# Routed experts of a two-layer decoder step: first unit taken out of the loop, tokens gathered by row instead of scattered by slot

## What is computed

```python
logits = jnp.einsum('bld,de->ble', h, router)
top_p, top_i = lax.top_k(softmax(logits), 2)      # weights made to sum to 1
for e in range(8):                                 # D_MODEL 1024, D_FF_EXPERT 1408
    out = out + combine[..., e:e+1] * swiglu(h, wg[e], wu[e], wd[e])
```

## Time and profile before

| | |
|---|---|
| median of 3 runs | 2325.3 us (2324.82 to 2325.86) |
| the profiled execution | 2321.99 us, span 2320.2 us |
| PE busy | 2076.9 us (90%), mean granted clock 0.951 |
| DVE busy | 1337.7 us (58%) |
| ACT busy | 942.0 us (41%) |
| POOL busy | 322.0 us (14%) |
| read from and written to DRAM | 384.07 MB and 43.47 MB |

### The profile page before, as it was taken

How to read it: one execution, slowest core, us unless ns; L and a number is a source line. 1 busy time by engine, 2 the same in 40 slices (tenths; PEclk the granted TensorE clock), 3 DMA queues, 4 the chain that set the end, 5 groups by cost and what they waited for, 6 DMA issues and landing times.

```text
span 2320.2 us, 38053 instructions
## 1 busy us (share of the span) xinstructions
PE 2076.9 (90%) x14026; PEld 1852.4 (80%) x14026; DVE 1337.7 (58%) x1712; ACT 942.0 (41%) x1085; POOL 322.0 (14%) x306
## 2 busy tenths in 40 slices
PE   4979999999799999979889999994499999999993
PEld 2868999998699999967789999893377777777772
DVE  2655665733533232246646566426488888888884
ACT  3321222343422122143212222524466767676664
POOL 2101212200000000001011222001221111122211
PEclk9988999999899999999989999997699999999997
DMA  8532222333922222226412232310799999998993
GB/s 317 201 127 64 96 77 98 113 138 135 401 90 88 79 86 94 87 90 242 155 55 82 90 108 91 119 51 33 301 340 357 358 355 363 362 365 336 345 357 134
DMA packets 117685, 428.31 MB, mean 185 GB/s; under 512 B 7792, under 2 KB 20400, under 8 KB 117120
## 3 DMA queue, kind: packets, MB, share of 16 engines
q1 hardware_dynamic: 90912, 323.43, 38.4%
q0 software_dynamic: 26720, 104.13, 12.2%
HBM read 384.07 MB, written 43.47 MB: 184 GB/s over the span
## 4 chain that ended last, share of the span: by engine, by line
PE 61%; issue 26%; DVE 4%; POOL 3%; ACT 2%; DMA 2%; DVEq 0%; POOLq 0%; SPq 0%; ACTq 0%
PE ps L1469 48%; PE ps L1493 3%; POOL wlr L605 3%; PE ps L1483 2%; PE ps L1584 1%; PE ps L1599 1%; PE ps L1580 1%; PE ps L1506 1%; DMA raw<-w_xbc 1%; PE ps L1595 1%; PE ps L1597 1%; PE ps L1554 1%; PE ps L1596 1%; POOL h_rows L595 0%; POOL rawr L613 0%
## 5 line engine op out<-in xcount | busy, mean ns | idle before, releaser
L1382 DVE TENSOR_TENSOR wlr<-rawr,whr 128x2048 fp32r<-128x2048 f32 (+2 forms) x216 | 476.6, 2221 | 92.6 <-ACT whr L844 92.4
L1469 PE MATMUL ps<-h_hi,whi 128*128 128x272 f32 x2368 | 499.2, 292 | 10.1 <-DVE h_lo L989 10.1
L1469 PE MATMUL ps<-h_lo,whi 128*128 128x272 f32 x2368 | 493.6, 290 | 0.0
L1469 PE MATMUL ps<-h_hi,wlo 128*128 128x272 f32 x2368 | 492.3, 289 | 0.0
L844 ACT CAST whr<-rawr 128x2048 fp32r<-128x2048 f32 (+1 forms) x240 | 382.1, 1606 | 183.2 <-DMA rawr<-w_gu 78.6
L1469 PEld LDWEIGHTS ps<-h_hi,whi 128*128 128x128 f32 x2368 | 375.0, 190 | 40.1 <-issue 39.9
L940 DVE TENSOR_TENSOR wlo<-raw,whi 128x1024 fp32r<-128x1024 f32 (+1 forms) x180 | 227.7, 1265 | 305.9 <-ACT whi L627 304.4
L1469 PEld LDWEIGHTS ps<-h_hi,wlo 128*128 128x128 f32 x2368 | 376.0, 190 | 0.0
L1469 PEld LDWEIGHTS ps<-h_lo,whi 128*128 128x128 f32 x2368 | 375.0, 190 | 0.0
L627 ACT CAST whi<-raw 128x1024 fp32r<-128x1024 f32 (+1 forms) x180 | 194.2, 1079 | 377.3 <-PE ps L1469 365.1
L1699 PE MATMUL ps<-whr,hu_hi 128*128 128x512 f32 (+1 forms) x576 | 224.3, 389 | 20.2 <-POOL wlr L605 14.6
(11 more groups left out here) (320 smaller groups left out, 2738.1 us busy)
## 6 DMA issues: line engine op xcount, KB each, us to landing
rawr<-w_gu SPq DMA_DIRECT2D x60, 2048.0 KB, 9.9
adaw<-w_ada POOLq DMA_DIRECT2D x48, 1024.0 KB, 7.8
rawr<-w_dn SPq DMA_DIRECT2D x24, 2048.0 KB, 7.9
raw<-w_mix SPq DMA_DIRECT2D x64, 512.0 KB, 3.4
raw<-w_gu SPq DMA_DIRECT2D x44, 512.0 KB, 3.4
rawr<-w_dn SPq DMA_DIRECT2D x12, 1536.0 KB, 9.8
raw<-w_out SPq DMA_DIRECT2D x32, 512.0 KB, 3.5
raw<-w_xbc SPq DMA_DIRECT2D x24, 512.0 KB, 3.8
```

The source lines that it names most:

```text
L1382: v.tensor_tensor(ring_group(wlr, g).rearrange("p k s c -> p s k c"), raw_group(g), ring_group(whr, g).bitcast(F32).rearrange("p k s c -> ...
L1469: ins = mm(ps[:, 2 * s + half, 0:HALF], w[:, s, k * P:(k + 1) * P], a[:, k, half * HALF:(half + 1) * HALF], start=(n < 2), stop=(n >= 6 * ...
```

## The change

The routed stage is rebuilt, and the slabs of the other stages are reordered:

- Loads get an explicit order and buffers: 0, 1, 2, 3, 4, the 1 MB load, the rest of the down weights, then the two down loads D0 and D1. The 1 MB load has a buffer of its own (`raw_half`); the others use three.
- Unit 0 is taken out of every engine's loop. The packing gives expert 0 at least one unit, so that unit 0 is always expert 0: SP loads its first three loads after the residual of the token mixer (x_ready), before the routing; ACT and DVE fill the ring's four slots before the loop.
- `htok` is stored as it is, by token, to `h_rows` (SP). DVE makes one-hot masks of the places, ten matmuls of PE turn them into a table `row_of` (which token is at each place of each unit), and POOL gathers each unit's 128 rows by one indirect read, from the table's column copied to `row_now`.
- POOL subtracts nothing any more: DVE makes the low parts of all 20 groups.
- The last turn of hidden values comes after group 13 instead of 15, the turn of the next unit's tokens after group 14 instead of 13.
- At the end the gathers of the earlier result of each token are issued before the last store, those of the later one after it, into separate tiles.
- `h_rows` is no longer zeroed, `y_rows` is zeroed in 17 pieces between the dense slabs of layer 0.
- `slab` waits for `whi`, does both products with `whi` for all rows, then waits for `wlo` and does the third.

```diff
...
+LOADS = (0, 1, 2, 3, 4, HALF_CHUNK, REST, D0, D1)
+BUFFER = {0: 0, 1: 1, 2: 2, 3: 0, 4: 1, HALF_CHUNK: RAWS, REST: 2, D0: 0, D1: 1}
+NTH = {0: 0, 3: 1, D0: 2, 1: 0, 4: 1, D1: 2, 2: 0, REST: 1, HALF_CHUNK: 0}
+PER_UNIT = (3, 3, 2, 1)
...
-ON_POOL = (6, 9)
...
-TURN_AFTER = {4: 0, 6: 1, 8: 2, 10: 3, 12: 4, 15: 5}
-TOKENS_AFTER = 13
...
+TURN_AFTER = {4: 0, 6: 1, 8: 2, 10: 3, 12: 4, 13: 5}
+TOKENS_AFTER = 14
...
+                    def load(u, e, i, first=False):
+                        from_load, of_last = before_load(i)
+                        split = last_group(from_load) + 1
+                        if not first:
+                            sp.wait_ge(grp_split, u * NGRP + (split if of_last else split + NGRP))
+                            if i == D0:
+                                sp.sem_inc(load_now, 1)
...
+                    sp.wait_ge(x_ready, (2 * L + 1) * KT)
+                    for i in LOADS[:RAWS]:
+                        load(0, 0, i, True)
+                    for c in range(NCH + 1):
+                        rows = CH if c < NCH else NS
+                        sp.wait_ge(rows_ready, c + 1)
+                        sp.dma_start(h_rows[c * CH:c * CH + rows, :], htok[0:rows, c, :]).then_inc(h_out, 16)
+                    for i in LOADS[RAWS:]:
+                        load(0, 0, i)
...
+                        pool.wait_ge(slabs_used, (FIRST[0]["exp"] + i) * 2 + PRIME)
+                        pool.dma_start(y_rows[i], zeros).then_inc(zero_out, 16)
...
+                def fetch_rows(value, column):
+
+                    pool.wait_ge(xu_turned, value)
+                    nc.gpsimd.tensor_copy(row_now[:, :], column).then_inc(row_copied, 1)
+                    pool.wait_ge(row_copied, value + 1)
+                    pool.sem_inc(fetch_now, 1)
+                    nc.gpsimd.indirect_dma_start(xu[:, :], None, h_rows,
+                                                 bass.IndirectOffsetOnAxis(ap=row_now[:, 0:1], axis=0)).then_inc(xu_in, 16)
...
+                pool.wait_ge(y_stored, n * 16 + 16)
+                pool.sem_inc(fetch_now, 1)
+                for c in LAST_ORDER:
+                    fetch_results(1, c)
                 pool.wait_ge(y_last, 16)
                 for c in LAST_ORDER:
-                    rows = CH if c < NCH else NS
-                    for s in range(2):
-                        nc.gpsimd.indirect_dma_start(
-                            y_got_tile(s, c)[0:rows], None, y_rows.rearrange("n p d -> (n p) d"),
-                            bass.IndirectOffsetOnAxis(ap=y_row[0:rows, s, c:c + 1], axis=0)).then_inc(y_got[c], 16)
+                    fetch_results(0, c)
...
+                    for g in range(RING):
+                        round_group(0, g)
+                    load_silu()
+                    rows_upper(1)
+                    body(0)
+                    act.wait_ge(table_ready, 1)
+                    n = act.value_load(units[0:1, 0:1], min_val=2, max_val=MAXU)
+                    with act.Fori(1, n) as u:
...
+                    link(v.tensor_scalar(n_units[:, 0:1], n_units[:, 0:1], 1.0, None, ALU.max))
...
+                    ten = slot[:, :, :].rearrange("p s c -> p (s c)")
+                    link(v.tensor_tensor(past, over(ten, MAXU + 1),
+                                         first_of[:, :].unsqueeze(1).broadcast_to([P, 2 * (NCH + 1), MAXU + 1]), ALU.is_ge))
+                    st.step(v.tensor_tensor(in_unit, past[:, :, 0:MAXU], past[:, :, 1:MAXU + 1], ALU.subtract))
+                    link(v.tensor_reduce(unit_no, past[:, :, 1:MAXU + 1], axis=AX_X, op=ALU.add))
+                    for s in range(2):
+                        of_s = in_unit[:, s * (NCH + 1):(s + 1) * (NCH + 1), :]
+                        st.step(v.tensor_tensor(of_s, of_s, over(token_id[:, :], MAXU), ALU.mult))
+                    link(v.scalar_tensor_tensor(unit_no, unit_no, -float(CAP), ten, ALU.mult, ALU.add))
+                    link(v.tensor_tensor(in_place, iota.unsqueeze(1).broadcast_to([P, 2 * (NCH + 1), CAP]),
+                                         over(unit_no, CAP), ALU.is_equal))
+                    v.memset(row_of[:, :], 0).then_inc(row_made, 1)
...
+                    dve.wait_ge(row_made, 2)
+                    v.tensor_copy(row_of[:, 0:MAXU], ps[:, 7, 256:256 + MAXU]).then_inc(row_ready, 1)
...
+                    for g in range(RING):
+                        split_group(0, g)
+                    rows_rest(1)
+                    body(0)
+                    coefficients(L, "post_ffn", 5, False)
+                    dve.wait_ge(table_ready, 1)
+                    n = dve.value_load(units[0:1, 0:1], min_val=2, max_val=MAXU)
+                    with dve.Fori(1, n) as u:
+                        for g in range(RING):
+                            split_group(u, g)
+                        body(u)
...
             def slab(m, s, kt, a_hi, a_lo, tile=None):
 
-                pe.wait_ge(lo_split, m * 2 + (s + 1 + PRIME))
+                pe.wait_ge(hi_split, m * 2 + (s + 1))
                 pe.wait_ge(taken[s], m + 1)
                 n = 0
                 for k in range(kt):
                     if tile:
 
                         pe.wait_ge(tile[0], tile[1] + k + 1)
-                    for w, a in ((whi, a_hi), (whi, a_lo), (wlo, a_hi)):
+                    for a in (a_hi, a_lo):
                         for half in range(2):
-                            ins = mm(ps[:, 2 * s + half, 0:HALF], w[:, s, k * P:(k + 1) * P],
-                                     a[:, k, half * HALF:(half + 1) * HALF], start=(n < 2), stop=(n >= 6 * kt - 2))
+                            mm(ps[:, 2 * s + half, 0:HALF], whi[:, s, k * P:(k + 1) * P],
+                               a[:, k, half * HALF:(half + 1) * HALF], start=(n < 2), stop=False)
                             n += 1
+                pe.wait_ge(lo_split, m * 2 + (s + 1 + PRIME))
+                for k in range(kt):
+                    for half in range(2):
+                        ins = mm(ps[:, 2 * s + half, 0:HALF], wlo[:, s, k * P:(k + 1) * P],
+                                 a_hi[:, k, half * HALF:(half + 1) * HALF], start=False, stop=(k == kt - 1))
                 ins.then_inc(slabs_used, 1)
...
+                for j in range(2 * (NCH + 1)):
+                    c = j % (NCH + 1)
+                    rows = CH if c < NCH else NS
+                    ins = mm(ps[:, 7, 256:256 + MAXU], in_place[0:rows, j, :], in_unit[0:rows, j, :], start=(j == 0),
+                             stop=(j == 2 * NCH + 1))
+                ins.then_inc(row_made, 1)
...
+                body(0)
+                pe.wait_ge(table_ready, 1)
+                n = pe.value_load(units[0:1, 0:1], min_val=2, max_val=MAXU)
+                with pe.Fori(1, n) as u:
+                    body(u)
...
```

More of the change, by code:

```diff
@@ L96, with last_group, before_load @@
 NGRP = len(GROUPS_OF)
-NSLOT, NCHUNK = 9, 6
-ON_POOL = (6, 9)
-N_POOL = len(ON_POOL)
-N_DVE = NGRP - N_POOL
-TURN_AFTER = {4: 0, 6: 1, 8: 2, 10: 3, 12: 4, 15: 5}
-TOKENS_AFTER = 13
[L103 to L113, removed]
+NCHUNK = 6
+TURN_AFTER = {4: 0, 6: 1, 8: 2, 10: 3, 12: 4, 13: 5}
+TOKENS_AFTER = 14
+assert NGRP % RING == 0
+def last_group(load):
+    return max(g for g, t in enumerate(GROUPS_OF) if t[1] == load)
+def before_load(load):
+    same = [x for x in LOADS if BUFFER[x] == BUFFER[load]]
+    return same[NTH[load] - 1], NTH[load] == 0
 class Tally:
@@ L493, in _ @@
+                        for i in LOADS:
+                            load(u, e, i)
+                            if i == 3:
                                 sp.wait_ge(y_taken, u * 2 + 2)
@@ new lines, in _ @@
+                pool.wait_ge(row_copied, 1)
+                nc.gpsimd.indirect_dma_start(xu[:, :], None, h_rows,
+                                             bass.IndirectOffsetOnAxis(ap=row_now[:, 0:1], axis=0)).then_inc(xu_in, 16)
+                fetch_rows(1, row_of[:, 1:2])
+                pool.wait_ge(table_ready, 1)
+                n = pool.value_load(units[0:1, 0:1], min_val=2, max_val=MAXU)
+                with pool.Fori(1, n) as u:
+                    fetch_rows(u + 1, row_of[:, bass.ds(u + 1, 1)])
@@ L891, in _ @@
                                 rows_upper(u + 2)
+                    for g in range(RING):
[6 more added lines that the diff above has]
+                    with act.Fori(1, n) as u:
+                        for g in range(3):
+                            round_group(u, g)
+                        act.wait_ge(y_stored, u * 16 + 16)
+                        act.wait_ge(grp_used, u * NGRP + 3)
+                        take_y(0)
+                        round_group(u, 3)
+                        act.wait_ge(grp_used, u * NGRP + 4)
+                        take_y(1)
+                        body(u)
                     act.wait_ge(y_stored, n * 16 + 16)
@@ L1407, in rows_rest, with body @@
                                         ).then_inc(hu_lo_ready, 1)
```

(23 more changed lines are left out.)

169 lines of the change are left out of this document (76 added, 93 removed).

## The result

The changed kernel takes 2291.61 us (median of four runs, 2290.68 to 2292.38), the kernel before in the same comparison 2325.06. The ratio is put at 0.9881 (95% interval 0.9861 to 0.9901), so 23 to 32 us less, where the prediction had 47.7 less and 2277.5. The two medians alone would give 0.9856; in later comparisons the kernel before ran at 2320.1 to 2320.3, which would give 0.9877. Kernels are therefore set side by side by their ratio to it. The two profiled executions have spans of 2320.2 and 2290.5 us: 29.7 us to be found.

A forecast was written before the change was run, and what follows sets the result against it. PE was taken to bound the routed stage, with two small holes per unit. Start 20.7, units 21, end 5 and slabs 2.5, minus 1.5 for leaving the peeled unit, made 47.7 us off: 2277.5 us, range 2262 to 2296.

The forecast's parts named there:

- Loads: Routed units: one queue emptying per unit, beat between 49.3 and 50.4, taken as 50.0; gain 21 us over 12 units.
- sign of being wrong: Routed units: PE waiting for DVE's splits or a turn after group 13 in every unit would show the forecast wrong.
- What is late next: Turn after group 13: its gate's product stands on DVE behind group 15's split, which needs D1; no size given.
- Rival 1: Routed stage: loads set the pace and the beat stays 51.75; 34.5 us off, 2291; chance 0.18.
- All low parts on DVE: Routed units: moving POOL's subtractions to DVE removes PE's first hole, 1.3 us per unit.
- The last turn: Routed units: splitting the last hidden values two groups earlier removes PE's second hole, 1.1 us per unit.
- PE's floor: Routed units: a unit without PE's two waits would take 49.3 us.
- The early gathers: Last unit: the other five result gathers run under it; no cost counted.
- Start: Start of the routed stage: first expert matmul at 1635.3 instead of 1656.0; gain 20.7 us, bounds 16 and 24.
- leaving the peeled unit: Between unit 0 and the loop: every queue reads the number of units; loss 1.5 us, bounds 0 and 2.
- End: After the last store: five gathers instead of ten remain; gain 5 us, bounds 0 and 6.8.
- Slabs: Dense slabs: beginning with whi saves one subtraction at each of two PE waits; gain 2.5 us, bounds 0 and 7.9.

The follow-up runs named there:

- e2: Changed kernel with the half-size gate and up load issued ahead of load 0 from the second unit on; ratio 0.9779, 2269.74 us, beat 49.39.
- e9: Changed kernel with the order and three buffers of the loads as in the kernel before; ratio 0.9786, beat 49.74 us.
- e5: Changed kernel with the last hidden columns' gate and product ahead of the rounding and split of group 15; ratio 0.9869, beat 51.08 us.
- e4: Changed kernel with half the bytes in every load from the second unit on; beat 48.28 us.
- e6: Changed kernel with the changes of e1, e2 and e5 together; ratio 0.9742, beat 48.74 us.
- e7: Kernel before with all subtractions on DVE and POOL's loop left out; ratio 0.993, beat 49.57 us.
- e8: Kernel before with half the bytes in every load of the routed stage; beat 49.37 us.
- e12: Changed kernel with the old order and buffers of loads and the old places of the last and tokens' turns; ratio 0.9792, beat 49.49 us.
- e1: Changed kernel with the five early result gathers issued only after the last unit's last load has landed; ratio 0.9861, 2287.13 us.
- e11: Kernel before with only the changed kernel's slabs; ratio 0.9986.
- e3: Changed kernel with the rest of the down weights loaded behind D0 instead of ahead of it; ratio 0.9942, beat 52.69 us.

## Why the prediction was wrong

*The step that failed* is "Loads". It saw the place ("the queue runs empty about once a unit there") and put it at "47.7 plus one emptying of 2.7 = 50.4", as a bound that the likeliest case, 50.0, stayed under; 51.24 was measured. The emptying costs 5.1 us and not 2.7: 2.7 is the excess of one landing over its transfer, whereas here load 0 can't be issued before D0, which holds its buffer, is rounded and split, and by then the queue has run dry. The other term was too high: 51.24 - 5.1 = 46.1, between the floor by bytes (45.1) and the one by share (47.7) that the prediction kept; with 47.7 the right emptying would have given 52.8. What the step left out is what used to run in that place: in the old order the 1.5 MB rest of the down weights is transferred while load 0 waits. The new order puts it ahead of D0 and D1, whose groups PE needs before it. Filling the gap with another load (e2) or putting the rest back (e9) recovers 1.85 and 1.5 us of the 51.24. The term was 21 us and measured 0, with the last unit in it.

One sign of being wrong that the prediction named came in every unit: PE waits for the turn after group 13 (8.0 us in ten units). It had been seen ("What is late next") and given no price; e5 shows that its own price is small, 0.16 us a unit: without it PE waits for splits instead, 21.4 us in ten units for 12.8.

*Rival 1* had nearly the time (2291). Its beat, 51.75, is near the measured one, and the loads do cost the changed kernel 2.96 us a unit (e4). That the time agrees is partly luck: it takes 34.5 us off, 28.5 of them for an earlier stream of loads, where the two profiled executions lie 29.7 apart and the start gave 18.9. The 3.3 us that were added for the median make up most of the difference. As a rate it is refuted: the same bytes go through in 48.74 us a unit in e6, at 377 GB/s over ten units, and at 380 in a unit of e9. The Trainium skill, DMA: Bandwidth & Descriptors (Where 436 GB/s comes from), holds about 358 GB/s to bind transfers from DRAM; the 359 of the changed kernel looks like it, but the rates of e6 and e9 show that it is not a cap here. The Trainium skill, HBM Reference (Specifications (TRN2)), which lets a core that streams alone go above its share, agrees with them.

*All low parts on DVE* was right and undersized: e7 alone gives 2.04 us a unit where the hole was read as 1.3. The hole was read from PE's waits alone, and the slow splits also held back loads (e7). *The last turn* was right for the engines: the floor falls from 49.37 (e8) to 48.28 (e4), of which 0.7 is the wait for the last hidden values that e8 still has, and undisturbed units from 49.2 (e12) to 48.2 (e9), 1.0 us where 1.1 was forecast; in the mean of all units it is not to be seen. So the beat went from 51.61 by 2.0 to some 49.6 (e7, e9 and e12), and the new order of the loads took 1.5 of it away again. "PE's floor" of 49.3 is 48.3 in the changed kernel: the same 2292 matmuls are booked at 491.6 us in it and at 482.2 in e4, so the busy time of a PE that waits holds some of its waiting.

*The early gathers* were the second miss: "the other five gathers run under the last unit" priced them at nothing. They cost 57.2 - 51.7 = 5.5 us (e1), about as much as the 4.9 to 5.7 that they save at the end.

*Start*: 18.9 for 20.7, read from the trace and not tested by a run; the 1.5 for leaving the peeled unit was not seen by itself. *End*: 4.9 for 5. *Slabs*: 5.9 in the changed kernel and 5.4 in e11 for 2.5, inside its bounds; the whole times of e11 allow 0 to 6, and why it is more than 2.5 was not tested.

## What to carry to other kernels

When a load is moved in a queue, price both places: whom it delays where it goes, and what the queue does where it was. Halving the bytes of every load is a cheap way to part the loads from the engines: here it gave the engines' floor in one run. It does not part a rate from an order; the same bytes in another order do (e2, e9). A wait of PE is not the whole price of a slow split: the split also holds a buffer, and with it the next load. Traffic that is put under a stage whose queue is full was paid for here by the next load that was due.

## What was not expected of the hardware

Around the 6.74 us in which PE stood in the last unit, and behind them, the granted clock was 0.69 and 0.74, so partly at the lower level of 1.2 GHz:

```profile
2228.00:2234.00 6.00, 1.20 (x3) 1.01 (x4) 3.02 (x3) 4.52 (x6) 0.00 (x0) 0.69 0.95 378
2234.00:2240.00 6.00, 6.00 (x23) 4.68 (x22) 5.85 (x7) 4.03 (x6) 0.00 (x0) 0.74 0.00 0
```

In e1, where PE is idle for 2.42 us in the whole last unit (51.72 - 49.30), that unit has 1.00 throughout; in e3, where PE waits up to 4.0 us at a time, the mean over ten units is 0.97. Of the 5.5 us by which the last unit is longer than in e1, 4.3 are idle time and 1.1 more busy time for the same 231 matmuls, so the stall cost something behind its end as well.

POOL's issue of an indirect read took 1.03 us at 1620.14, ahead of DVE's splits, and up to 2.78 us at 2207.34 beside them; at 2212.71, while DVE stood idle, it took 0.95. No run tests this alone.
